# First four modulation halves of a macaron DiT kernel: rounded part and remainder under a four-column stationary, in place of float32 matmuls

## The reference

```python
mod_l = (jax.nn.silu(c) @ w_ada[l] + b_ada[l]).reshape(b_, 1, N_MOD, D_MODEL)
mod_c = (jax.nn.silu(c_ctx) @ w_ada[l] + b_ada[l]).reshape(N_MOD, D_MODEL)
...
def _pre(x, nw, shift, scale):
    return rmsnorm(x, nw) * (1 + scale) + shift
```

## Time and profile before

| | us |
|---|---|
| median of three runs | 3045.71 |
| profiled execution | 3045.91 |
| its span (first to last instruction) | 3044.0 |
| TensorE busy (matmul) | 2776.2 |
| VectorE busy | 1457.6 |
| ScalarE busy | 836.9 |
| TensorE's share of the chain that ended last | 81% |
| mean granted TensorE clock | 0.961 of full |

### The profile page before, as it was taken

How to read it: one execution, slowest core, us unless ns; L and a number is a source line. 1 busy time by engine, 2 the same in 40 slices (tenths; PEclk the granted TensorE clock), 3 DMA queues, 4 the chain that set the end, 5 groups by cost and what they waited for, 6 DMA issues and landing times.

```text
span 3044.0 us, 35860 instructions
## 1 busy us (share of the span) xinstructions
PE 2776.2 (91%) x14352; PEld 2466.9 (81%) x14352; DVE 1457.6 (48%) x1975; ACT 836.9 (27%) x1128; POOL 84.7 (3%) x40
## 2 busy tenths in 40 slices
PE   5999999898988869999998899999997978599997
PEld 2999997777866769999887799999777756488876
DVE  2454555465344555545465555542455555532232
ACT  3211112443322331111134311111343523322222
POOL 0000000000000010000000100000001000100001
PEclk9999999998988989999999999999998999699999
DMA  6233334322200213333342233332332301222221
GB/s 225 70 111 133 114 114 159 113 98 87 77 1 1 97 56 111 119 130 110 117 170 101 96 110 110 122 113 69 124 111 88 104 1 42 83 97 96 96 83 69
DMA packets 98664, 298.95 MB, mean 98 GB/s; under 512 B 6672, under 2 KB 23056, under 8 KB 87056
## 3 DMA queue, kind: packets, MB, share of 16 engines
q1 hardware_dynamic: 91440, 280.42, 26.8%
q10 hardware_dynamic: 7136, 17.30, 1.6%
HBM read 295.60 MB, written 2.10 MB: 98 GB/s over the span
## 4 chain that ended last, share of the span: by engine, by line
PE 81%; DVE 8%; ACT 4%; issue 4%; POOL 1%; DMA 1%; SPq 0%; POOLq 0%; DVEq 0%; ACTq 0%
PE ps L1424 44%; PE ps L1443 20%; PE ps L760 5%; PE ps L867 2%; PE ps L1453 2%; POOL x L1007 1%; ACT w_hi L1022 1%; DVE arena L1269 1%; PE ps L1482 1%; PE ps L1492 1%; PE ps L850 1%; PE ps L841 1%; DVE w_lo L1184 1%; DVE arena L1294 1%; PE ps L903 1%
## 5 line engine op out<-in xcount | busy, mean ns | idle before, releaser
L1424 PE MATMUL ps<-xn_hi,w_hi 128*128 128x384 f32 (+2 forms) x2496 | 706.4, 345 | 33.2 <-DVE xn_lo L1262 19.6
L1424 PE MATMUL ps<-xn_lo,w_hi 128*128 128x384 f32 (+2 forms) x2496 | 701.9, 343 | 0.0
L1424 PE MATMUL ps<-xn_hi,w_lo 128*128 128x384 f32 (+2 forms) x2496 | 701.5, 343 | 0.0
L1184 DVE TENSOR_TENSOR w_lo<-raw,w_hi 128x2048 fp32r<-128x2048 f32 x195 | 444.8, 2281 | 203.1 <-ACT w_hi L1022 203.0
L1424 PEld LDWEIGHTS ps<-xn_hi,w_hi 128*128 128x128 f32 x2496 | 459.1, 190 | 47.7 <-DVE xn_lo L1262 20.7
L1424 PEld LDWEIGHTS ps<-xn_lo,w_hi 128*128 128x128 f32 x2496 | 460.4, 190 | 12.5
L1424 PEld LDWEIGHTS ps<-xn_hi,w_lo 128*128 128x128 f32 x2496 | 459.9, 190 | 12.5
L1022 ACT ACTIVATE w_hi<-raw 128x2048 fp32r<-128x2048 f32 x195 | 369.1, 1893 | 32.2 <-DMA raw<-w_ff_in 21.3
L1443 PE MATMUL ps<-w_hi,hj_hi 128*128 128x512 f32 x952 | 306.7, 404 | 71.3 <-DVE hj_lo L1192 59.9
L1210 DVE SCALAR_TENSOR_TENSOR acc<-raw_ada,silu_c,acc 128x512 f32<-128x512 f32 x512 | 345.5, 746 | 4.6 <-DVE acc L1198 3.2
L1137 ACT ACTIVATE arena<-ps 128x384 f32 (+1 forms) x132 | 57.6, 489 | 913.1 <-PE ps L1424 913.1
(11 more groups left out here) (190 smaller groups left out, 2383.0 us busy)
## 6 DMA issues: line engine op xcount, KB each, us to landing
raw<-w_ff_in SPq DMA_DIRECT2D x88, 1024.0 KB, 5.5
raw<-w_ff_out SPq DMA_DIRECT2D x77, 1024.0 KB, 5.0
raw_ada<-w_ada SPq DMA_DIRECT2D x128, 512.0 KB, 3.7
raw<-w_out SPq DMA_DIRECT2D x16, 1024.0 KB, 4.8
raw<-w_in SPq DMA_DIRECT2D x12, 1024.0 KB, 5.3
arena<-w_ada SPq DMA_DIRECT2D x4, 2048.0 KB, 17.4
gate_row<-norm_w ACTq DMA_DIRECT2D x12, 512.0 KB, 4.2
arena<-dft_l_in ACTq DMA_DIRECT2D x2, 2048.0 KB, 8.1
```

What stands on the lines that cost most here:

```text
L1184: nc.vector.tensor_tensor(w_lo[par][:, 0:width], raw[par][:, 0:width], w_hi[par][:, 0:width].bitcast(F32), ALU.subtract).then_inc(S["w_lo" ...
L1424: ins = mm(ps[:, 4 * b + 2 * g + c, col:col + wd], w[:, k, c, :], xx[:, k, t0:t0 + wd], start=(k == 0 and i == 0), stop=(k == KC - 1 and i ...
```

## The change

The four halves are loaded in eight quarters of 1 MB (four k slices each), each with its own semaphore. VectorE makes of each quarter a rounded copy and the remainder, which is written in place of the quarter. `silu_c` too is split, into four columns: rounded c and c_ctx, remainder of both. TensorE multiplies the four-column stationary with the rounded and then with the remainder quarter, which gives four rows of 512, and adds the rounded and the remainder rows by a matmul with `pair_sum` (4x2) in place of the transposes. The SP queue issues only `cvec` ahead of the quarters, `b_col` and `nw_col` go to the ACT queue ahead of `x`, the other five constants behind the quarters. `mask` moves behind the last `prenorm_lo`.

```diff
@@ buffers @@
+        ada_r = inner.enter_context(nc.sbuf_tensor("ada_r", [P, XN], F32R))
+        inner.enter_context(nc.sbuf_tensor("ada_gap", [P, A_TRI + 2 * P - XN], F32))
+        ada_r3 = inner.enter_context(nc.sbuf_tensor("ada_r3", [P, KC * HB + 2 * SLOT], F32R))
...
+        silu_hl = sb("silu_hl", [P, KC, 4], F32R)
+        pair_sum = sb("pair_sum", [P, 2])
...
+        def ada0_hi(i, q):
+            if i % 2 == 0:
+                quarter = ada_r3[:, KC * HB + q * SLOT:KC * HB + (q + 1) * SLOT]
+            else:
+                quarter = (w_hi[1], w_lo[1])[q][:]
+            return quarter.rearrange("p (k n) -> p k n", k=KC // 2)
+        def ada0_lo(i):
+            part = ada_r[:, i * KC * HB:(i + 1) * KC * HB] if i < 3 else ada_r3[:, 0:KC * HB]
+            return part.rearrange("p (k n) -> p k n", k=KC)
@@ SP queue @@
-            for dst, src in ((cvec[:], cvec_in), (b_col[:], b_col_in), (nw_col[:], nw_col_in), (convw[:], convw_in),
-                             (convb[:], convb_in), (hn_w[:], hn_w_in), (tri, tri_in), (gate_b[:], gate_b_in)):
-                sp.dma_start(dst, src).then_inc(S["consts"], 16)
+            sp.dma_start(cvec[:], cvec_in).then_inc(S["cvec_in"], 16)
             for i in range(4):
                 if i == 3:
                     load(0, 0, w_ff_in[0, 0, 0])
                 src = w_ada[0].rearrange("(k p) n -> p k n", p=P)[:, :, i * HB:(i + 1) * HB]
-                sp.dma_start(ada0(i), src).then_inc(S["ada_first"][i], 16)
+                for q in range(2):
+                    ks = slice(q * KC // 2, (q + 1) * KC // 2)
+                    sp.dma_start(ada0(i)[:, ks], src[:, ks]).then_inc(S["ada_first"][2 * i + q], 16)
+            for dst, src in ((convw[:], convw_in), (convb[:], convb_in), (hn_w[:], hn_w_in), (tri, tri_in),
+                             (gate_b[:], gate_b_in)):
+                sp.dma_start(dst, src).then_inc(S["consts"], 16)
@@ ScalarE and the ACT queue @@
+            for dst, src in ((b_col[:], b_col_in), (nw_col[:], nw_col_in)):
+                act.dma_start(dst, src).then_inc(S["cols_in"], 16)
             for t in range(NT):
                 act.dma_start(x[:, t, :], x_in[t]).then_inc(S["x_in"], 16)
-            act.wait_ge(S["consts"], 16 * 8)
+            act.wait_ge(S["cvec_in"], 16)
@@ VectorE @@
+            def first_split(i, q):
+                ks = slice(q * KC // 2, (q + 1) * KC // 2)
+                part = ada0(i)[:, ks]
+                dve.wait_ge(S["ada_first"][2 * i + q], 16)
+                if i >= 2:
+                    dve.wait_ge(S["rows_mm"], i - 1)
+                nc.vector.tensor_copy(ada0_hi(i, q), part).then_inc(S["ada0_hi"], 1)
+                dve.wait_ge(S["ada0_hi"], 2 * i + q + 1)
+                nc.vector.tensor_tensor(ada0_lo(i)[:, ks], part, ada0_hi(i, q).bitcast(F32), ALU.subtract).then_inc(S["ada0_lo"], 1)
+            def first_col(i):
+                dve.wait_ge(S["rows_mm"], i + 1)
+                nc.vector.tensor_copy(acc[0:4, i % 2, :], ps[0:4, 5, :]).then_inc(S["rows_sb"], 1)
...
-            for t in range(NT):
-                prenorm_rs(t, t)
+            dve.wait_ge(S["silu_c"], 1)
+            own.link(nc.vector.tensor_copy(silu_hl[:, :, 0:2], silu_c[:]))
+            nc.vector.tensor_tensor(silu_hl[:, :, 2:4], silu_c[:], silu_hl[:, :, 0:2].bitcast(F32), ALU.subtract).then_inc(S["silu_hl"], 1)
             for i in range(4):
-                dve.wait_ge(S["rows_mm"], i + 1)
-                nc.vector.tensor_copy(acc[0:2, i % 2, :], ps[0:2, 5, :]).then_inc(S["rows_sb"], 1)
+                first_split(i, 0)
+                if i == 0:
+                    dve.wait_ge(S["cols_in"], 32)
+                else:
+                    first_col(i - 1)
+                    finish_col(i - 1, i - 1, 6)
+                first_split(i, 1)
+                if i == 0:
+                    for t in range(NT):
+                        prenorm_rs(t, t)
                 if i == 2:
                     split_w(0, 0)
-                finish_col(i, i, 6)
+            first_col(3)
+            finish_col(3, 3, 6)
...
+            dve.wait_ge(S["consts"], 16 * 5)
+            nc.vector.tensor_scalar(mask[:], tri, -1.0, -NEG, ALU.add, ALU.mult).then_inc(S["dve_consts"], 1)
@@ TensorE @@
             for i in range(4):
-                pe.wait_ge(S["ada_first"][i], 16)
-                for k in range(KC):
-                    ins = mm(ps[0:2, 5, :], silu_c[:, k, :], ada0(i)[:, k, :], start=(k == 0), stop=(k == KC - 1))
+                if i:
+                    pe.wait_ge(S["rows_sb"], i)
+                for q in range(2):
+                    pe.wait_ge(S["ada0_hi"], 2 * i + q + 1)
+                    for k in range(KC // 2):
+                        mm(ps[0:4, 5, :], silu_hl[:, q * KC // 2 + k, :], ada0_hi(i, q)[:, k, :], start=(q == 0 and k == 0), stop=False)
+                    pe.wait_ge(S["ada0_lo"], 2 * i + q + 1)
+                    for k in range(q * KC // 2, (q + 1) * KC // 2):
+                        ins = mm(ps[0:4, 5, :], silu_hl[:, k, :], ada0_lo(i)[:, k, :], start=False, stop=(k == KC - 1))
...
                 for c in range(4):
-                    ins = nc.tensor.transpose(ps[:, 6, GW + 2 * c:GW + 2 * c + 2], acc[0:2, i % 2, c * P:(c + 1) * P], ident[0:2, 0:2])
+                    ins = mm(ps[:, 6, GW + 2 * c:GW + 2 * c + 2], acc[0:4, i % 2, c * P:(c + 1) * P], pair_sum[0:4, :],
+                             start=True, stop=True)
```

More of the change, by code:

```diff
@@ L173, in build @@
         inner.close()
+        ada_r = inner.enter_context(nc.sbuf_tensor("ada_r", [P, XN], F32R))
+        inner.enter_context(nc.sbuf_tensor("ada_gap", [P, A_TRI + 2 * P - XN], F32))
+        ada_r3 = inner.enter_context(nc.sbuf_tensor("ada_r3", [P, KC * HB + 2 * SLOT], F32R))
+        inner.close()
         arena = sb("arena", [P, XN + 2 * HG])
@@ L289, in build @@
         for name in (
-            "consts pool_consts dve_consts x_in "
+            "cvec_in cols_in consts pool_consts dve_consts x_in "
             "w_raw0 w_raw1 w_hi w_lo w_used "
-            "ada_raw0 ada_raw1 ada_used fin_mm fin_read row_mm row_read silu_c "
+            "ada_raw0 ada_raw1 ada_used fin_mm fin_read row_mm row_read silu_c silu_hl ada0_hi ada0_lo "
             "silu h_done hj_hi hj_lo "
@@ L300, in build @@
             S[name] = ctx.enter_context(nc.semaphore("s_" + name))
-        S["ada_first"] = [ctx.enter_context(nc.semaphore(f"s_ada_first{i}")) for i in range(4)]
+        S["ada_first"] = [ctx.enter_context(nc.semaphore(f"s_ada_first{i}")) for i in range(8)]
         N_SLOTS = SUBS[-1]["slot"] + SUBS[-1]["in_slots"] + SUBS[-1]["k_slots"]
@@ L834, in maxima @@
             def maxima(h, d):
+                pe.wait_ge(S["dve_consts"], 1)
                 for g in range(2):
@@ L1302, in first_out @@
                     hj(sub, 0, c, sub["hj"] + c, 2 * nb + c, c)
-            dve.wait_ge(S["consts"], 16 * 8)
+            def first_split(i, q):
[10 more added lines that the diff above has]
+                nc.vector.tensor_copy(acc[0:4, i % 2, :], ps[0:4, 5, :]).then_inc(S["rows_sb"], 1)
             dve.wait_ge(S["pool_consts"], 2)
             nc.vector.tensor_copy(ident_bf[:], ident[:])
-            nc.vector.tensor_scalar(mask[:], tri, -1.0, -NEG, ALU.add, ALU.mult).then_inc(S["dve_consts"], 1)
-            for t in range(NT):
-                prenorm_rs(t, t)
+            nc.vector.tensor_tensor(pair_sum[0:4, :], ident[0:4, 0:2], ident[0:4, 2:4], ALU.add)
+            dve.wait_ge(S["silu_c"], 1)
+            own.link(nc.vector.tensor_copy(silu_hl[:, :, 0:2], silu_c[:]))
+            nc.vector.tensor_tensor(silu_hl[:, :, 2:4], silu_c[:], silu_hl[:, :, 0:2].bitcast(F32), ALU.subtract).then_inc(S["silu_hl"], 1)
             for i in range(4):
-                dve.wait_ge(S["rows_mm"], i + 1)
-                nc.vector.tensor_copy(acc[0:2, i % 2, :], ps[0:2, 5, :]).then_inc(S["rows_sb"], 1)
+                first_split(i, 0)
[8 more added lines that the diff above has]
+                        prenorm_rs(t, t)
                 if i == 2:
                     split_w(0, 0)
-                finish_col(i, i, 6)
+            first_col(3)
+            finish_col(3, 3, 6)
             make_mod(0, 0)
@@ L1485, in _ @@
             pe.wait_ge(S["pool_consts"], 2)
-            pe.wait_ge(S["dve_consts"], 1)
-            pe.wait_ge(S["silu_c"], 1)
+            pe.wait_ge(S["silu_hl"], 1)
             for i in range(4):
-                pe.wait_ge(S["ada_first"][i], 16)
-                for k in range(KC):
-                    ins = mm(ps[0:2, 5, :], silu_c[:, k, :], ada0(i)[:, k, :], start=(k == 0), stop=(k == KC - 1))
+                if i:
[7 more added lines that the diff above has]
+                        ins = mm(ps[0:4, 5, :], silu_hl[:, k, :], ada0_lo(i)[:, k, :], start=False, stop=(k == KC - 1))
                 ins.then_inc(S["rows_mm"], 1)
```

## The result

Slower: 3060.02 us (six runs, 3058.96 to 3060.84) against 3045.27 for the kernel before beside it, a ratio of 1.0049 with a 95% interval of 1.0037 to 1.006. The forecast was 3050.8, in a range that ended at 3057.0. The profiled execution took 3059.73, its span is 3057.9, 13.9 longer than before.

The account below looks back on a forecast made before the run. TensorE was taken to bound the kernel before, VectorE the start of the changed one. A later M added 5.0 to 3045.9 us, giving 3050.9, stated as 3050.8; range 3046.0 to 3057.0.

Parts of the forecast that it names:

- the sum: Whole kernel: profiled 3045.9 us plus 5.0 at M; landing within +2 to +7 was given 0.62.
- M: End of the fourth finish_col, the last vecs write; forecast at 57.7 us against 52.73 before.
- VectorE becomes the bound, through the reciprocals: Start of kernel: six quarters queue behind reciprocals ending at 27.1; VectorE needs 8.4 us a half against today's 8.13.
- rival B: VectorE's rounded copy runs at the two-source rate, 2.3 us; +11.4, total 3057; chance 0.13.
- The four small matmuls with `pair_sum` take the place of four transposes of the same form: nothing, give or take 0.2.: After each half's products on TensorE: swapping transposes for matmuls costs nothing, give or take 0.2 us.
- Wrong if VectorE waits for TensorE or a load in the six quarters: Sign that would refute the forecast, in VectorE's six quarters behind the reciprocals; no size given.
- When `x` lands: Loads at the start: w_ada packets alternate with x's, delaying x by 4.8 us to 17.3; bounds 13.3 to 21.4.
- C: Start loads: w_ada gets half the bytes or ACT issues queue; x at 21.4, total 3055; decides past 18.5; chance 0.14.
- TensorE's tail and its clock: Last half before M: TensorE ends at 56.3, between 55.1 at full clock and 57.2 at 1.2 GHz.
- All that follows depends on M by fixed steps.: Transposes, prenorm_mod and first projection behind M move with it by fixed steps; no further gain or loss.
- E, no gain: Whole kernel: a real gain would need reciprocals not ahead of the quarters; no mechanism seen; chance 0.03.

Follow-up runs that it names:

- E2: Changed kernel with the six prenorm_rs reciprocals moved behind split (1,1) instead of (0,1); 3049.38 us, ratio 1.0018 to the kernel before.
- E3: Changed kernel with two-row transposes for the pair_sum matmuls, leaving out products of silu_c's remainder rows; 3052.51 us, ratio 1.0025 to the kernel before.
- E1: Changed kernel with the old issue order: eight constants first on the SP queue, x first on ACT; 3055.24 us, ratio 1.0035 to the kernel before.
- E9: Changed kernel with each w_ada quarter issued as two loads of 256 columns, giving 1024-byte packets; 3061.49 us, one run.
- E4: Kernel before with five dependent 128x2048 VectorE subtractions ahead of make_mod as delay; 3054.65 us, ratio 1.0035 to the kernel before.
- E8: Changed kernel with two dependent 128x2048 VectorE subtractions ahead of make_mod as delay; 3063.56 us, ratio 1.0056 to the kernel before.
- E6: Changed kernel with E5's four-row transposes and E2's later reciprocals together; 3042.53 us, ratio 0.9989 to the kernel before.
- E7: E6 with ScalarE making the rounded copies of halves 2 and 3, w_lo of slot 0 behind the first prenorm_lo; 3042.83 us, ratio 0.9985.
- E12: E7 run again unchanged; 3041.82 us, ratio 0.9983 to the kernel before.
- E5: Changed kernel with four-row transposes and a second VectorE add in place of the pair_sum matmuls; 3051.76 us, ratio 1.0018 to the kernel before.
- E10: Changed kernel with twelve additional TensorE matmuls a half into an unused bank; 3060.17 us, ratio 1.0041 to the kernel before.

## Why the prediction was wrong

The profiled execution took 8.8 us more than the sum's 3050.9. Of that 5.9 lies ahead of M and 2.9 behind it.

- *VectorE becomes the bound, through the reciprocals.* Right: the changed kernel's chain runs over `x` and the reciprocals, and E2 takes 9.3 off M by moving them. Its copy was put at 1.24 and took 1.22; rival B (2.3) is out. The Trainium skill (VectorE: DVE Perf Modes, "The perf-mode tier table") gives 1.227 us for such a copy: the trace agrees, with 1.21 to 1.23. (One reading was off without harm: the first of the four halves took 9.96 before, only the other three 8.13.)
- *"The four small matmuls with `pair_sum` take the place of four transposes of the same form: nothing, give or take 0.2."* **This step failed, and it is the largest term.** They are not of the same form. VectorE waits for all of it: 1.31 more in each of three halves and 0.6 in the last, 4.5 us. The prediction's own sign, "Wrong if VectorE waits for TensorE or a load in the six quarters", came, with three waits of 1.95 us. The profile of before could have said so: its eight float32 matmuls of L1492 stood there as sixteen rows, its four transposes as four:

```profile
27.71 0.41 PE ps L1498 x4
```

- *When `x` lands.* 17.3 forecast, 19.05 measured, inside the bounds of 13.3 to 21.4, +1.75. That is past the 18.5 which was to decide for C, but the packets (703 to 732) speak against C: the sign could not tell sharing by bytes from a late start of `x`. The rule (packet by packet) was right for these packets. The sum of bytes was short: by 19.05 the loads had moved 6.5 MB, where by 12.5 they had moved 3.9 in the kernel before, 2.6 more and not 1.85. By 6.0 us, when `x` began to move, the SP queue had moved 1.1 MB, where 0.5 MB were allowed for.
- *TensorE's tail and its clock.* 2.1 forecast between VectorE's last remainder and the end of half 3, 1.66 measured: -0.4. The clock was low and rose within half 3, as taken.
- Together 4.5 + 1.75 - 0.4 = 5.9, the whole of M's error. With the tail of E3 in mind, the terms don't add freely: without the small matmuls TensorE sets the tail and 0.5 of the gain is lost.
- *"All that follows depends on M by fixed steps."* Right for the first 41 us. Behind them it was a figure without an uncertainty, and that is its fault: most profiles wander by -3 to +3 us against a rigid shift, E1's by 9.8 and E9's by 7.6, and with them the time at the low clock (table above). The medians lie above the shift of M more often than below it (2.4 to 3.8 for the changed kernel). Whether a part of that belongs to a later M as such is open. E4 and E8 were too coarse to tell. A range with ±3 for this stretch would have ended at 3060.0, level with the measured 3060.02.
- *E, no gain.* Right for this order of the code. E6, E7 and E12 show that the idea itself pays once the reciprocals stand later and the small matmuls go.

## What to carry to other kernels

Work that is given to an idle engine inherits everything that stands ahead of it in that engine's order: look for tiny instructions that wait for someone else (here six reciprocals of 0.16 us held back six quarters, 21 us of work, until 28.9, though the first of these had landed by 19.7) before counting its idle time as room. When a transpose becomes a matmul, even one of four rows by two columns, count its passes and weight loads, since in a chain of small steps the smallest is paid at full length. And when loads are moved ahead of each other, count who shares with whom: the queues here shared by packets, so loads issued earlier on one queue made those of the other late.

## What the runs showed of the hardware

- Four float32 matmuls with a stationary of 4x128 and two moving columns: 1.88 us at the low clock, 1.06 at the full one. Four float32 transposes of the same four rows: 0.58 and 0.41 (E5).
- Two queues with 4096-byte and 2048-byte packets alternated 703 to 732; with 1024-byte packets 783 to 1126. Sharing packet by packet doesn't hold for all sizes.
- A VectorE copy of 128x2048 within SBUF from float32 to rounded float32 takes 1.22, just over half of the 2.29 of the subtraction.
- TensorE worked in the changed kernel in bursts between waits of 2 to 14 us, and its granted clock changed eight times in the first 60 us (low from 15.2 to 18.6, 22.0 to 39.1, 42.5 to 49.3 and 52.7 to 59.6). Keeping it busy with other matmuls raised the clock (E10: full from 40 to 56) and cost more than it gave (M at 66.5, not 63.6).
- Over fourteen profiles the time at the low clock behind 125 us was 222 to 249 us, and a profile's surplus behind M grew with it, from -3 to +10 us.
